# Router rows and expert rows kept as f16 halves and turned by DMA instead of by TensorE

## The chip, the cores and the metric

The kernel runs on one core of a Trainium2 chip. The metric is device time in microseconds (us) from start to end of one execution. Engines are named as in the profile: PE is TensorE's matmul stream and PEld its weight loads, DVE is VectorE, ACT is ScalarE, POOL is GpSimd, SP is SyncE. SP issues most of the plain DMAs; POOL issues the indirect ones.

## What is computed

One decoder layer over 4096 tokens of width 1024: attention and convolution heads with an output projection, then a channel mixer with top-1 of 4 groups and top-2 of 8 experts. The part that the change touches is how the normalized row `hn` of each token reaches the router and the experts.

```
h = h + mixed @ w_out[l]
hn = rms_norm(h, ffn_norm_g[l])
...
g_prob = softmax(xf @ w_gr + b_gr);  g_p, g_idx = top_k(g_prob, 1)
e_logits = einsum('td,dge->tge', xf, w_er) + b_er     # xf is hn in float32
e_val, e_idx = top_k(e_logits of the chosen group, 2)
...
# tokens sorted by expert, in blocks of 128 rows that belong to one expert
def expert_block(args):
    xb, e = args
    return (silu(xb @ w_g[e]) * (xb @ w_u[e])) @ w_d[e]
```

## The kernel before

The kernel has two stages. `mixer` goes over 32 tiles of 128 tokens (loop variable t) and ends with routing; `experts` goes over the blocks of 128 gathered rows (loop variable b), expert by expert. Products keep nearly float32 precision by splitting both factors into a high and a low half and adding three products (hi*hi, hi*lo, lo*hi): f16 halves in the mixer (`split_mm`, L412), fp32r halves in the experts (L1333).

TensorE contracts over the partitions, so every activation has to be turned (transposed) first: 128 tokens on the partitions become 128 features on the partitions. Before the change each turn is made by PE, as four transposes of 128x128 into one PSUM bank, read by ACT for the high half and by DVE for the low half.

**Mixer.** Each engine's program is one `body(t)` written by hand, and its order is the program order. PE's body runs: turn x (psE, psF, L448), scores (psA to psD, L464), router product of the previous tile (psH, 16 small matmuls, L477), q projection (psG), turn the probabilities (L495), k and v (psH), probabilities times V (L520), C projection (psF), H projection (psC), turn a and yc (L535), output projection (psD, psE), counts (L554, L555), B projection (psG), turn k (L568), turn q (psF, psB, L578), turn `hn` (psC, psD, L588). `hn` is made by DVE (L1138) from h (L1134) and a statistic of ACT (L738 to L600). The turned `hn` goes as f16 halves to `both_hnT` (in `wo_all`; ACT L755, DVE L1154), which the router product of the next pass reads. SP stores `hn` as float32 rows of 4 KB in `hn_dram` (L397).

**Experts.** For block b, POOL loads the slot numbers (L1289), gathers the 128 rows from `hn_dram` into `xg` (L1257), and later adds the finished block into the output (`scatter`, L1269). PE's `block_` runs: gate (psA, 24 matmuls), turn of the previous block's activations (psE, L1348), up (psB, 24), turn of the next block's rows (psC, psD, L1341), down of the previous block (psF, psG, 12 each). ACT and DVE share one outline, `halves`: where a new expert begins, split its gate weights; scale the finished block into y; split the up weights; `turn` (halves of the activations); `act_stage` (ACT silu L1440, DVE product L1483); `turn_x` (halves of the next block's rows, ACT L1453, DVE L1493, once `up` has read the old ones); split the down weights. A weight matrix is split in 8 pieces (ACT L1427, DVE L1469), and the gate matmuls of an expert's first block follow the pieces one by one. SP reloads each raw weight buffer (2 MB) once both engines have split it. `hold(eng, sem)` is an increment of a semaphore that nobody waits for.

POOL may overwrite `xg` once PE has turned it (`xgT_ps`), and `scatter(b)` waits for both halves of y and for the last scatter to have landed.

## Time and profile before

| | us |
|---|---|
| median of 3 runs | 2934.15 |
| lowest and highest | 2933.95, 2938.82 |
| profiled execution, its time | 2933.64 |
| profiled execution, its span | 2932.0 |

The span runs from the first to the last instruction of the trace; 1.6 us of the profiled execution's time lie around it. Up to about 1480 us the mixer runs, from about 1500 us the experts. Times in the rows are microseconds from the start of the span unless marked ns. A matmul row's own duration overlaps the next one, so the distance between starts tells what it costs PE.

### The profile page before, as it was taken

Reading aid. Unit: us, or ns where it says so; the run is one execution under the profiler, and the core shown is the slowest. Engines: PE = TensorE matmul, PEld = TensorE weight load, DVE = VectorE, ACT = ScalarE, POOL = GpSimd, SP = SyncE. Lnnn points to the kernel's source line nnn. Section 1 sums busy time; section 2 is a strip of 40 time slices with the busy share of each in tenths; the row PEclk is TensorE's granted clock in tenths of the full one; section 3 lists DMA queues with packets and bytes.
Section 4 is the critical chain, followed back from the end, with each engine's and each line's share of the span. In section 5 each row is a group of like instructions: output and inputs, shape, how many; then the busy total and the mean of one; then the engine's idle time right before and its main releaser. Section 6 shows DMA issues by size and latency. Waiting matters only on the chain. (4 is left out here: it accounts for less than half of the span.)

```text
span 2932.0 us, 51902 instructions
## 1 busy us (share of the span) xinstructions
PE 2833.6 (97%) x15862; PEld 2015.1 (69%) x15863; DVE 1685.4 (57%) x4102; ACT 1424.0 (49%) x3174; POOL 809.2 (28%) x826
## 2 busy tenths in 40 slices
PE   4999999999999999999859999999999999999998
PEld 2565566556556656655538888888888888888886
DVE  5566666666666666666643546645564545356543
ACT  6655454555455455545423445544454444345433
POOL 1122223313222221321212323323322323333222
PEclk9899999999999999999979999999999999999999
DMA  8112112111211211221335667766776756657763
GB/s 291 40 69 79 57 61 79 66 63 68 79 53 65 79 64 57 75 78 50 140 111 162 183 196 222 237 200 195 233 243 194 229 150 197 180 170 232 241 189 57
DMA packets 152747, 398.52 MB, mean 136 GB/s; under 512 B 18027, under 2 KB 18188, under 8 KB 151692
## 3 DMA queue, kind: packets, MB, share of 16 engines
q1 hardware_dynamic: 123868, 309.36, 30.6%
q0 software_dynamic: 28848, 88.77, 13.0%
q8 instruction: 16, 0.26, 0.0%
q14 instruction: 15, 0.12, 0.0%
HBM read 310.20 MB, written 87.88 MB: 136 GB/s over the span
## 5 line engine op out<-in xcount | busy, mean ns | idle before, releaser
L412 PE MATMUL psG<-wi_all,xT_hi 128*128 128x512 f16 x1024 | 308.1, 383 | 0.7 <-DVE xT_lo L944 0.7
L1333 PE MATMUL psB<-up_hi,gT_hi 128*128 128x512 f32 x632 | 254.2, 402 | 0.0
L1333 PE MATMUL psA<-gate_hi,gT_hi 128*128 128x512 f32 x632 | 246.6, 390 | 3.1 <-ACT gT_hi L1453 1.7
L1333 PE MATMUL psB<-up_hi,gT_lo 128*128 128x512 f32 x632 | 247.4, 391 | 0.0
L1257 POOL DMA_INDIRECT xg<-hn_rows,slots x80 | 98.2, 1228 | 539.7 <-DMA slots<-slot_table 394.2
L1333 PE MATMUL psA<-gate_hi,gT_lo 128*128 128x512 f32 x632 | 246.7, 390 | 0.0
L1333 PE MATMUL psA<-gate_lo,gT_hi 128*128 128x512 f32 x632 | 246.3, 390 | 0.0
L1333 PE MATMUL psB<-up_lo,gT_hi 128*128 128x512 f32 x632 | 246.2, 390 | 0.0
L1469 DVE TENSOR_TENSOR down_lo<-wi_all,down_hi 128x512 fp32r<-128x512 f32 x256 | 157.0, 685 | 147.3 <-ACT down_hi L1427 147.3
L1453 ACT ACTIVATE gT_hi<-psC 128x512 fp32r<-128x512 f32 x80 | 47.8, 598 | 383.1 <-PE psC L1341 383.1
L1483 DVE TENSOR_TENSOR act_rows<-psB,gated 128x512 f32<-128x512 f32 x79 | 54.7, 692 | 289.6 <-PE psB L1333 289.6
L837 POOL DMA_INDIRECT slot_table<-entry,slot x64 | 64.8, 1013 | 562.5 <-DVE tok L1126 535.2
L1427 ACT ACTIVATE down_hi<-wi_all 128x512 fp32r<-128x512 f32 x256 | 137.0, 619 | 149.4 <-PE psG L1333 149.4
L738 ACT ACTIVATE dump<-h 128x1024 bf16<-128x1024 f32 x32 | 33.8, 1057 | 339.0 <-DVE h L1134 339.0
L1266 POOL COPY rows_of_y<-slots 128x1 int32<-128x1 int32 x80 | 129.4, 1617 | 247.7 <-DVE y L1476 246.9
L412 PE MATMUL psG<-wi_all,xT_lo 128*128 128x512 f16 x512 | 195.8, 382 | 0.0
L1469 DVE TENSOR_TENSOR gate_lo<-wi_all,gate_hi 128x512 fp32r<-128x512 f32 x256 | 157.0, 685 | 46.0 <-ACT gate_hi L1427 46.0
L412 PEld LDWEIGHTS psG<-wi_all,xT_hi 128*128 128x128 f16 x1024 | 98.7, 98 | 117.3 <-issue 4.5
L652 ACT ACTIVATE prob<-prob,soft 128x256 f32<-128x256 f32 x256 | 127.9, 500 | 80.5 <-DVE soft L976 74.9
L412 PE MATMUL psF<-wi_all,xT_hi 128*128 128x512 f16 x528 | 157.4, 380 | 4.6 <-DVE wi_all L936 4.6
L412 PE MATMUL psC<-wi_all,xT_hi 128*128 128x512 f16 x528 | 157.5, 380 | 0.0
L1469 DVE TENSOR_TENSOR up_lo<-wi_all,up_hi 128x512 fp32r<-128x512 f32 x256 | 156.7, 683 | 1.0 <-ACT up_hi L1427 1.0
(343 smaller groups left out, 7174.9 us busy)
## 6 DMA issues: line engine op xcount, KB each, us to landing
wi_all<-in_w_gate SPq DMA_DIRECT2D x32, 2048.0 KB, 9.4
wi_all<-in_w_up SPq DMA_DIRECT2D x32, 2048.0 KB, 12.8
wi_all<-in_w_down SPq DMA_DIRECT2D x32, 2048.0 KB, 9.2
xt<-in_x SPq DMA_DIRECT2D x32, 512.0 KB, 3.3
um<-u_rows SPq DMA_DIRECT2D x64, 256.0 KB, 2.7
xres<-in_x SPq DMA_DIRECT2D x32, 512.0 KB, 4.1
out_rows<-h SPq DMA_DIRECT2D x32, 512.0 KB, 2.6
hn_rows<-hn SPq DMA_DIRECT2D x32, 512.0 KB, 2.6
```

Source lines behind the costliest of these rows:

```text
L412: m = nc.tensor.matmul(ps, left[l][:, k, :], weights.half(r, k, n, width), start=(k == 0 and j == 0), stop=(k == KD - 1 and j == 2))
L652: s.activation(prob[:, hd, :], prob[:, hd, :], ACT.Exp, bias=ntop[:, hd:hd + 1], accum_out=psum_[:, hd:hd + 1]).then_inc(p_sb.sem, 1)
L738: s.activation(dump[:], h[:], ACT.Square, accum_out=ss_h).then_inc(h_rs.sem, 1)
L837: g.indirect_dma_start(table, bass.IndirectOffsetOnAxis(ap=slot[:, n:n + 1], axis=0), entry[:, n, :], None, bounds_check=E * CAP - 1).then ...
L1257: pool.indirect_dma_start(xg[:], None, hn_dram, bass.IndirectOffsetOnAxis(ap=slots[:, 0, 0:1], axis=0), bounds_check=SEQ + P - 1).then_inc ...
L1266: g.tensor_copy(rows_of_y[:], slots[:, 3, 0:1]).then_inc(named, 1)
L1333: m = nc.tensor.matmul(ps[:, :], l[:, k, :], r[:, r_k[n], :], start=(n == 0 and j == 0), stop=(n == len(l_k) - 1 and j == 2))
L1427: s.activation(hi[n][:, k, :], raw[n][:, k, :], ACT.Copy).then_inc(hi_s[n], 1)
L1453: s.activation(gT_hi[:, 4 * h:4 * h + 4, :].rearrange("p k c -> p (k c)"), ps[:, :], ACT.Copy).then_inc(xgT_hi, 1)
L1469: v.tensor_tensor(lo[n][:, k, :], raw[n][:, k, :], hi[n][:, k, :].bitcast(F32), ALU.subtract).then_inc(lo_s[n], 1)
L1483: v.tensor_tensor(act_rows[:], psB[:, :], gated[:], ALU.mult).then_inc(act_s, 1)
```

## The change

It removes PE's turn of `hn` in the mixer and of the gathered rows in the experts, with the two PSUM reads that followed each, and lets DMA transposes do both, on f16 halves.

- **Mixer, ACT and DVE:** after `hn`, ACT writes its f16 high half over all 1024 columns (into the bytes of `a`), and DVE then the low half (into the bytes of `Cs`). `hn` itself moves behind the k and q copies on DVE; ACT's copy of B (`Bs`) moves behind q and the high half.
- **Mixer, SP:** in place of the store of `hn`, two DMA transposes (high, then low) into `both_hnT`, then two stores of 256 KB each, so a row of `hn_dram` is still 4 KB but holds 1024 high and 1024 low halves. DVE's write of `a` and ACT's write of `Cs` in the next pass wait for all four.
- **Mixer, PE:** the turn of `hn` goes; the turns of k and q come ahead of the B projection; the router product goes behind the q projection and waits for the transposes (`hnT_in`).
- **Experts:** `turn_rows` on ACT, between `turn` and `act_stage`, waits for the gather of the next block and issues two DMA transposes (high, low) from `xg` into `both_gT16`. `turn_x` waits for them (`turned`) and is now one operation of 1024 columns on each engine: ACT scales the high half into `gT_hi`, DVE the low half into `gT_lo`, no longer one after the other. POOL waits for `turned` before it overwrites `xg`.
- One semaphore `held` takes the place of three. `inv_hn` is the inverse of the scale of the halves.

The core of the diff:

```diff
@@ -231,7 +233,7 @@
     mT_hi, mT_lo = sb("mT_hi", [P, KD, P], F16), sb("mT_lo", [P, KD, P], F16)
     h, hn = sb("h", [P, D]), sb("hn", [P, D])
     both_hnT = w_out_split.spare(KD * P).bitcast(F16).rearrange("p (a k c) -> p a k c", a=2, k=KD)
-    hnT_hi, hnT_lo = both_hnT[:, 0], both_hnT[:, 1]
+    hn_hi, hn_lo = a[:].bitcast(F16), Cs[:].bitcast(F16)
...
@@ -393,10 +396,18 @@
             if live(t, 1):
                 after(sp, h_s, t)
                 sp.dma_start(out[bass.ds((t - 1) * P, P), :], h[:]).then_inc(rows_out.sem, 16)
-                after(sp, hn_s, t)
-                sp.dma_start(hn_dram[bass.ds((t - 1) * P, P), :], hn[:]).then_inc(rows_out.sem, 16)
+                after(sp, lg_ps, t - 1)
+                after(sp, hn_hi_s, t)
+                hold(sp, held)
+                sp.dma_start_transpose(both_hnT[:, 0], hn_hi).then_inc(hnT_in.sem, 16)
+                after(sp, hn_lo_s, t)
+                hold(sp, held)
+                sp.dma_start_transpose(both_hnT[:, 1], hn_lo).then_inc(hnT_in.sem, 16)
+                for half, rows in enumerate((a, Cs)):
+                    sp.dma_start(hn_dram[bass.ds((t - 1) * P, P), half * CC:(half + 1) * CC], rows[:]).then_inc(halves_out.sem, 16)
         schedule(sp, body)
         after(sp, rows_out, TILES)
+        after(sp, halves_out, TILES)
 
     @block.tensor
     def _(pe):
...
@@ -456,8 +467,10 @@
 
                     if j == 1:
                         after(pe, qT_dve, t)
-                    if j >= 2:
-                        after(pe, hT_dve, t - 1, j - 1)
+                    if j == 2:
+                        after(pe, u_s, t)
+                    if j == 3:
+                        after(pe, h_s, t - 1, 1)
                     for i in range(2):
                         hd = 2 * j + i
                         for half in range(2):
@@ -468,9 +481,17 @@
                             m = nc.tensor.matmul(ps[:, i * 256:(i + 1) * 256], cst[0:1, C_ONE:C_ONE + P],
                                                  pad_mask, start=False, stop=True)
                     m.then_inc(s_ps.sem, 1)
+            if full:
+                after(pe, b_sb, t)
+                after(pe, xTl, t + 1, 1)
+                split_mm(psG[:, :], xT, "in", 0, False, range(KD // 2))
+            if proj:
+                after(pe, xTl, t + 1)
+            if full:
+                split_mm(psG[:, :], xT, "in", 0, False, range(KD // 2, KD)).then_inc(pq.sem, 1)
             if route:
 
-                after(pe, hT_dve, t - 1)
+                after(pe, hnT_in, t - 1)
                 for k in range(KD):
 
                     for half in ((0, 1) if k < KD - 1 else (1, 0)):
...
@@ -478,14 +499,6 @@
                                              w_rt16[:, k, 0:2 - half, :].rearrange("p a n -> p (a n)"),
                                              start=(k == 0 and half == 0), stop=(k == KD - 1 and half == 0))
                 m.then_inc(lg_ps.sem, 1)
-            if full:
-                after(pe, b_sb, t)
-                after(pe, xTl, t + 1, 1)
-                split_mm(psG[:, :], xT, "in", 0, False, range(KD // 2))
-            if proj:
...
@@ -578,15 +587,10 @@
                         m = nc.tensor.transpose(ps[:, c * P:(c + 1) * P],
                                                 q2[:, 4 * b + c, :, :].rearrange("p a d -> p (a d)").bitcast(F32), ident)
                     m.then_inc(qT_ps.sem, 1)
-            if attn:
-                after(pe, hn_s, t)
-                if proj:
-                    after(pe, u_s, t + 1)
-                for b, ps in enumerate((psC, psD)):
-                    for c in range(4):
-                        k = 4 * b + c
-                        m = nc.tensor.transpose(ps[:, c * P:(c + 1) * P], hn[:, k * P:(k + 1) * P], ident)
-                    m.then_inc(hT_ps.sem, 1)
+            if full:
+                after(pe, q_sq, t + 1)
+                after(pe, q_n, t + 1)
+                split_mm(psG[:, :], xT, "in", O_B).then_inc(pb.sem, 1)
         schedule(pe, body)
...
@@ -707,6 +711,8 @@
             if proj:
                 after(act, pc, t + 1)
                 after(act, u_s, t)
+                after(act, hnT_in, t - 1)
+                after(act, halves_out, t - 1)
                 s.activation(Cs[:], psF[:, :], ACT.Copy, scale=inv_in).then_inc(c_sb.sem, 1)
             if isinstance(t, int) and t == 0:
                 split_hi("out", FIRST_CHUNKS)
@@ -740,20 +746,19 @@
                 after(act, hn_s, t - 1)
                 rstd(h_rs, t, ss_h, ln1[3], r_h, D)
             if full:
+                after(act, qT_ps, t + 1, 1)
+                after(act, s_ps, t)
+                s.activation(qT[:, 0:4 * P], psF[:, :], ACT.Copy).then_inc(qT_act.sem, 1)
+            if attn:
+                after(act, hn_s, t)
+                after(act, mT_ps, t, 1)
+                s.activation(hn_hi, hn[:], ACT.Copy, scale=hn_scale).then_inc(hn_hi_s.sem, 1)
+            if full:
                 after(act, pb, t + 1)
                 after(act, cv, t)
                 if isinstance(t, int) and t == 0:
                     act.wait_ge(band_out, 16 * len(band_places))
                 s.activation(Bs[:], psG[:, :], ACT.Copy, scale=inv_in).then_inc(b_sb.sem, 1)
-                after(act, qT_ps, t + 1, 1)
-                after(act, s_ps, t)
-                s.activation(qT[:, 0:4 * P], psF[:, :], ACT.Copy).then_inc(qT_act.sem, 1)
-            if attn:
-                after(act, lg_ps, t - 1)
-                for b, ps in enumerate((psC, psD)):
-                    after(act, hT_ps, t, b + 1)
-                    s.activation(hnT_hi[:, 4 * b:4 * b + 4, :].rearrange("p k c -> p (k c)"), ps[:, :], ACT.Copy,
-                                 scale=hn_scale).then_inc(hT_act.sem, 1)
             if isinstance(t, int) and t == -2:
                 bounds("in")
...
@@ -1027,6 +1032,8 @@
                 after(dve, o_ps, t)
                 after(dve, den_s, t)
                 after(dve, mT_ps, t - 1)
+                after(dve, hnT_in, t - 1)
+                after(dve, halves_out, t - 1)
                 a_heads = a[:].rearrange("p (h d) -> p h d", h=HEADS)
                 for kv, ps in enumerate((psE, psA)):
                     o = ps[:, :].rearrange("p (h a d) -> p h a d", h=4, a=2)
@@ -1132,10 +1139,6 @@
                     after(dve, h_ps, t, n + 1)
                     c = slice(n * 512, (n + 1) * 512)
                     v.scalar_tensor_tensor(h[:, c], ps[:, :], inv_out, xres[:, c], ALU.mult, ALU.add).then_inc(h_s.sem, 1)
-                after(dve, h_s, t)
-                after(dve, h_rs, t)
-                after(dve, hT_ps, t - 1)
-                v.scalar_tensor_tensor(hn[:], h[:], r_h, g_ffn[:], ALU.mult, ALU.mult).then_inc(hn_s.sem, 1)
             if full:
                 after(dve, k_prev, t + 1)
             if proj:
...
-                for b, ps in enumerate((psC, psD)):
-                    after(dve, hT_act, t, b + 1)
-                    v.scalar_tensor_tensor(hnT_lo[:, 4 * b:4 * b + 4, :].rearrange("p k c -> p (k c)"), ps[:, :], hn_scale,
-                                           hnT_hi[:, 4 * b:4 * b + 4, :].rearrange("p k c -> p (k c)"),
-                                           ALU.mult, ALU.subtract).then_inc(hT_dve.sem, 1)
+                after(dve, h_s, t)
+                after(dve, h_rs, t)
+                after(dve, hn_hi_s, t - 1)
+                v.scalar_tensor_tensor(hn[:], h[:], r_h, g_ffn[:], ALU.mult, ALU.mult).then_inc(hn_s.sem, 1)
+                if proj:
+                    after(dve, u_s, t + 1)
+                after(dve, hn_hi_s, t)
+                v.scalar_tensor_tensor(hn_lo, hn[:], hn_scale, hn_hi, ALU.mult, ALU.subtract).then_inc(hn_lo_s.sem, 1)
 
         schedule(dve, body)
 
         steps = [0]
-        last = sig("last").sem
...
@@ -1198,6 +1203,9 @@
     hi = {n: sb(f"{n}_hi", [P, 8, 512], F32R) for n in raw}
     lo = {n: sb(f"{n}_lo", [P, 8, 512], F32R) for n in raw}
     xg = sb("xg", [P, D])
+    rows_hi, rows_lo = (xg[:, h * DE:(h + 1) * DE].bitcast(F16) for h in range(2))
+
+    both_gT16 = wi_flat[:, 3 * 4096:3 * 4096 + KD * P].bitcast(F16).rearrange("p (a k c) -> p a k c", a=2, k=KD)
     gT_hi, gT_lo = sb("gT_hi", [P, KD, P], F32R), sb("gT_lo", [P, KD, P], F32R)
     gated, act_rows = sb("gated", [P, DE]), sb("act_rows", [P, DE])
...
@@ -1289,7 +1297,7 @@
             pool.dma_start(slots[:, 0, :], table[bass.ds(e * CAP + i * P, P), :]).then_inc(slots_in, 16)
             pool.wait_ge(slots_in, 16 * (b + 1))
             if not (isinstance(b, int) and b == 0):
-                pool.wait_ge(xgT_ps, 2 * b)
+                pool.wait_ge(turned, 32 * b)
                 hold(pool, held)
             gather()
...
@@ -1334,13 +1342,6 @@
                                          stop=(n == len(l_k) - 1 and j == 2))
             return m
 
-        def transpose_rows(b):
-            pe.wait_ge(rows_in, 16 * (b + 1))
-            for h, ps in enumerate((psC, psD)):
-                for c in range(4):
-                    m = nc.tensor.transpose(ps[:, c * P:(c + 1) * P], xg[:, (4 * h + c) * P:(4 * h + c + 1) * P], ident)
-                m.then_inc(xgT_ps, 1)
-
         def turn_act(b):
 
...
                 turn_act(b)
             split_mm(psB, range(KD), (gT_hi, gT_lo), (hi["up"], lo["up"]), list(range(KD)), first, "up", e
                      ).then_inc(up_ps, 1)
-            transpose_rows(b + 1)
             if not static0:
 
...
                 turn(b)
+            if turn_rows:
+                turn_rows(b + 1)
             act_stage(b)
             turn_x(b + 1)
...
@@ -1445,18 +1448,26 @@
             act.wait_ge(y_ps, 2 * b + 2)
             s.activation(aT_hi[:].rearrange("p k c -> p (k c)"), psE[:, :], ACT.Copy).then_inc(aT_hi_s, 1)
 
+        def turn_rows(b):
+
+            act.wait_ge(rows_in, 16 * (b + 1))
+            if not (isinstance(b, int) and b == 0):
+                act.wait_ge(xgT_hi, b)
+                act.wait_ge(xgT_lo, b)
+            for half, rows in enumerate((rows_hi, rows_lo)):
+                hold(act, held)
+                act.dma_start_transpose(both_gT16[:, half], rows).then_inc(turned, 16)
+
         def turn_x(b):
             if not (isinstance(b, int) and b == 0):
                 act.wait_ge(up_ps, b)
-            for h, ps in enumerate((psC, psD)):
-                act.wait_ge(xgT_ps, 2 * b + h + 1)
-                s.activation(gT_hi[:, 4 * h:4 * h + 4, :].rearrange("p k c -> p (k c)"), ps[:, :],
-                             ACT.Copy).then_inc(xgT_hi, 1)
+            act.wait_ge(turned, 32 * (b + 1))
+            s.activation(gT_hi[:], both_gT16[:, 0], ACT.Copy, scale=inv_hn[:]).then_inc(xgT_hi, 1)
 
...
         def turn_x(b):
-            for h, ps in enumerate((psC, psD)):
-                dve.wait_ge(xgT_hi, 2 * b + h + 1)
-                v.tensor_tensor(gT_lo[:, 4 * h:4 * h + 4, :].rearrange("p k c -> p (k c)"), ps[:, :],
-                                gT_hi[:, 4 * h:4 * h + 4, :].rearrange("p k c -> p (k c)").bitcast(F32),
-                                ALU.subtract).then_inc(xgT_lo, 1)
+            if not (isinstance(b, int) and b == 0):
+                dve.wait_ge(up_ps, b)
+            dve.wait_ge(turned, 32 * (b + 1))
+            v.tensor_scalar(gT_lo[:], both_gT16[:, 1], inv_hn[:], None, ALU.mult).then_inc(xgT_lo, 1)
 
```

What stands in a row on three engines. PE in the mixer, end of the tile loop: `wo_all` is the output projection's weight and `wi_all` the input projection's, `q` and `kn` are normalized queries and keys. Before, and then after:

```order
L412 MATMUL psG<-wi_all,xT_lo 128x512
L130 REGISTER_ALU
L568 MATMUL psH<-cst,kn 128x128 x2
L578 MATMUL psF<-cst,q 128x128 x4
L578 MATMUL psB<-cst,q 128x128 x4
L588 MATMUL psC<-cst,hn 128x128 x4
L588 MATMUL psD<-cst,hn 128x128 x4
```

```order
L423 MATMUL psE<-wo_all,mT_lo 128x512
L130 REGISTER_ALU
L577 MATMUL psH<-cst,kn 128x128 x2
L587 MATMUL psF<-cst,q 128x128 x4
L587 MATMUL psB<-cst,q 128x128 x4
L423 MATMUL psG<-wi_all,xT_hi 128x512 x2
L423 MATMUL psG<-wi_all,xT_lo 128x512
```

The eight transposes of `hn` are gone, and the B projection (psG) now comes last in the tile, right ahead of the next tile's turn of x.

PE in the experts, the end of `up` and the start of `down` in a block that opens an expert; before, and then after:

```order
L1333 MATMUL psB<-up_hi,gT_lo 128x512
L1338 ISA
L1341 MATMUL psC<-cst,xg 128x128 x4
L1341 MATMUL psD<-cst,xg 128x128 x4
L1333 MATMUL psF<-down_hi,aT_hi 128x512
```

```order
L1341 MATMUL psB<-up_hi,gT_hi 128x512
L1341 MATMUL psB<-up_lo,gT_hi 128x512
L1341 MATMUL psB<-up_hi,gT_lo 128x512
L1356 REGISTER_ALU
L1341 MATMUL psF<-down_hi,aT_hi 128x512
```

The turn of the next block's rows between the two products is gone.

ACT in the same block, from the up weights to the down weights; before, and then after:

```order
L1427 ACTIVATE up_hi<-wi_all 128x512 x8
L1445 REGISTER_ALU
L1446 ACTIVATE aT_hi<-psE 128x512
L1437 REGISTER_ALU
L1440 ACTIVATE gated<-psA 128x512
L1452 ISA
L1453 ACTIVATE gT_hi<-psC 128x512
L1452 REGISTER_ALU
L1453 ACTIVATE gT_hi<-psD 128x512
L1409 REGISTER_ALU
L1427 ACTIVATE down_hi<-wi_all 128x512 x8
```

```order
L1430 ACTIVATE up_hi<-wi_all 128x512 x8
L1448 REGISTER_ALU
L1449 ACTIVATE aT_hi<-psE 128x512
L1453 REGISTER_ALU
L1455 REGISTER_ALU
L1459 DMA_TRANSPOSE wi_all<-xg 128x8x128 x2
L1443 ACTIVATE gated<-psA 128x512
L1464 REGISTER_ALU
L1465 ACTIVATE gT_hi<-wi_all,inv_hn 128x1024
L1410 REGISTER_ALU
L1430 ACTIVATE down_hi<-wi_all 128x512 x8
```

Two DMA transposes stand between the halves of the activations and the silu, and one wide copy takes the place of two.

## Rows read from the trace of the kernel before

**Rows 1.** The page, part 1: busy us, share of the span, instructions.

```profile
PE 2833.6 (97%) x15862; PEld 2015.1 (69%) x15863; DVE 1685.4 (57%) x4102; ACT 1424.0 (49%) x3174; POOL 809.2 (28%) x826
```

**Rows 2.** Windows (mixer, experts): length, busy us per engine, PE clock, DMA share, GB/s.

```profile
200.00:627.00 427.00, 427.00 (x2820) 254.95 (x2817) 276.32 (x877) 225.90 (x597) 111.74 (x100) 1.00 0.18 68
1980.00:2445.00 465.00, 465.00 (x2209) 386.67 (x2207) 247.60 (x395) 212.18 (x395) 144.55 (x160) 1.00 0.71 211
```

**Rows 3.** Chain of waits, one block of the experts: start us, us, what.

```profile
2167.12 5.44 PE psA L1333 x24
...
2173.00 5.49 PE psB L1333 x24
2178.49 0.44 PE psC L1341 x4
...
2179.37 2.75 PE psF L1333 x12
...
2184.84 1.36 PE psA L1333 x6
```

**Rows 4.** Timeline, end of one mixer tile: start us, us, engine, instruction, idle before.

```profile
708.17 1.61 DVE L1138 SCALAR_TENSOR_TENSOR hn<-h,stat,g_ffn 128x1024 f32<-128x1024 f32 x1 [1.84 <-ACT stat L600]
...
710.77 0.69 ACT L747 ACTIVATE Bs<-psG,scale_w 128x512 f32<-128x512 f32 x1 [2.68 <-PE psG L412]
...
711.66 0.60 PE L588 MATMUL psC<-cst,hn 128*128 128x128 f32 x4
...
712.53 0.60 PE L448 MATMUL psE<-cst,xt 128*128 128x128 f32 x4
...
715.32 0.63 PE L477 MATMUL psH<-w_rt,wo_all 128*128 128x72 f16 x16
...
715.80 0.59 PE L412 MATMUL psG<-wi_all,xT_hi 128*128 128x512 f16 x2
```

**Rows 5.** DMA issues: queue, count, KB each, median us to landing.

```profile
u_rows<-u SPq DMA_DIRECT2D x33, 256.0 KB, 2.0
...
xg<-hn_rows,slots POOLq DMA_INDIRECT x80, 4.5
out_rows<-y,rows_of_y POOLq DMA_INDIRECT x80, 9.7
```

**Rows 6.** Groups by line: instructions, busy us, mean ns, idle before, releaser.

```profile
L588 PE MATMUL psC<-cst,hn 128*128 128x128 f32 x128 | 19.3, 273 | 4.0 <-DVE hn L1138 4.0
L738 ACT ACTIVATE dump<-h 128x1024 bf16<-128x1024 f32 x32 | 33.8, 1057 | 339.0 <-DVE h L1134 339.0
```

**Rows 7.** Timeline, experts: ACT, DVE and POOL.

```profile
1779.72 1.11 POOL L1257 DMA_INDIRECT xg<-hn_rows,slots  x1 [7.66 <-DMA slots<-slot_table]
...
2173.12 0.60 ACT L1446 ACTIVATE aT_hi<-psE 128x512 fp32r<-128x512 f32 x1 [1.10 <-PE psE L1348]
...
2181.61 4.28 ACT L1427 ACTIVATE gate_hi<-wi_all 128x512 fp32r<-128x512 f32 x8 [1.55 <-issue]
...
2182.53 4.91 DVE L1469 TENSOR_TENSOR gate_lo<-wi_all,gate_hi 128x512 fp32r<-128x512 f32 x8 [1.64 <-ACT gate_hi L1427]
...
2185.20 1.37 POOL L1257 DMA_INDIRECT xg<-hn_rows,slots  x1 [6.60 <-DMA slots<-slot_table]
```

**Rows 8.** Chain of waits, the block in which the 1779.72 gather falls.

```profile
1777.19 5.44 PE psA L1333 x24
```

**Rows 9.** Issues of the down weights on SP: ns min/median/max, first and last start.

```profile
L170 SPq DMA_DIRECT2D wi_all<-in_w_down x32: 372/373/4075, 1442.3 to 2846.3; - x32
```

**Rows 10.** Timeline, the last tile's turn and router product.

```profile
1478.45 0.66 PE L588 MATMUL psC<-cst,hn 128*128 128x128 f32 x4 [3.96 <-DVE hn L1138]
...
1481.43 0.90 PE L477 MATMUL psH<-w_rt,wo_all 128*128 128x72 f16 x16 [1.57 <-DVE wo_all L1154]
```

**Rows 11.** Chain of waits, first gathered rows to first gate product.

```profile
1510.38 1.11 PE psC L1341 x4
...
1513.81 1.62 PE psA L1333 x3
```

More of the change, by code:

```diff
@@ L488, in body @@
                 split_mm(psG[:, :], xT, "in", 0, False, range(KD // 2, KD)).then_inc(pq.sem, 1)
+            if route:
+                after(pe, hnT_in, t - 1)
+                for k in range(KD):
+                    for half in ((0, 1) if k < KD - 1 else (1, 0)):
+                        m = nc.tensor.matmul(psH[:, 256:256 + (2 - half) * RT], both_hnT[:, half, k, :],
+                                             w_rt16[:, k, 0:2 - half, :].rearrange("p a n -> p (a n)"),
+                                             start=(k == 0 and half == 0), stop=(k == KD - 1 and half == 0))
+                m.then_inc(lg_ps.sem, 1)
             if attn:
@@ L823, in body @@
                     after(pool, v_cur, t)
-                    hold(pool, pool_held)
+                    hold(pool, held)
                     g.tensor_copy(V[:, 0, :], V[:, 1, :]).then_inc(v_prev.sem, 1)
@@ L827, in body @@
                 after(pool, v_st, t + 1)
-                hold(pool, pool_held)
+                hold(pool, held)
                 g.tensor_copy(V[:, 1, :], vst[:]).then_inc(v_cur.sem, 1)
@@ L834, in body @@
                 after(pool, rt2, t - 1)
-                hold(pool, pool_held)
+                hold(pool, held)
                 for n in range(2):
@@ L968, in body @@
                     after(dve, s_ps, t, j + 1)
-                    hold(dve, dve_held)
+                    hold(dve, held)
                     for i in range(2):
@@ L1187, in experts @@
 def experts(nc, ctx, env):
-    out, table, hn_dram, cst, ident, blocks_of, raw, raw_in, load_expert = (env[n] for n in (
-        "out table hn_dram cst ident blocks_of raw raw_in load_expert").split())
+    out, table, hn_dram, cst, ident, blocks_of, inv_hn, held, wi_flat, raw, raw_in, load_expert = (env[n] for n in (
+        "out table hn_dram cst ident blocks_of inv_hn held wi_flat raw raw_in load_expert").split())
     psA, psB, psC, psD, psE, psF, psG = (env[f"ps{c}"] for c in "ABCDEFG")
```

44 lines of the change are left out of this document (19 added, 25 removed).

## The prediction

> **What bounds the kernel now.** I read the busy shares first: PE is busy for 97% of the span, no other compute engine for more than 57% [rows 1]. The windows say whether that holds stage by stage: in a mixer stretch of 427 us PE is busy for 427.00, in an experts stretch of 465 us for 465.00, at full clock [rows 2]. PE has no gap, so each matmul taken away shortens the run, as long as nothing that hung on it comes late. What must not come late is read from the chain of waits and the timelines.
>
> The chain of one block of the experts is PE alone: gate, turn of the activations, up, turn of the next rows, down; from one gate to the next it is 2184.84 - 2167.12 = 17.72 us [rows 3]. The turn of the next rows takes 2179.37 - 2178.49 = 0.88 us of them. In the mixer the turn of `hn` takes 712.53 - 711.66 = 0.87 us of a tile, and PE goes on without a gap [rows 4].
>
> **What is removed.** The experts have 80 turns of rows, one per gather [rows 5]; the first of them is waited for and is costed below with the start. 79 x 0.88 = 69.5 us lie in the chain. The mixer has 128 transposes into psC, four a tile, so 32 turns [rows 6]; the last is exposed and goes below too. 31 x 0.87 = 27.0 us. The PSUM reads that followed on ACT and DVE are replaced by wide operations and were beside PE's work.
>
> **What the DMA transposes need in the experts.** A transpose of 256 KB is not in this trace. I call X the time from the issue of the pair to the landing of both. Nearest rows: a plain store of 256 KB lands in 2.0 us, the gather of 512 KB into SBUF, in the same stretch beside the weight loads, in 4.5, the scatter that adds 512 KB in 9.7 [rows 5]. So 2.0 to 9.7; I take 4.5, since the gather moves the bytes of a pair to the same side, beside the same loads.
>
> When is the pair issued? It stands on ACT behind `turn`, which starts 2173.12 - 2167.12 = 6.0 after the gate's start and takes 0.6 [rows 7]. It also waits for the gather: in one block that was issued 0.4 after the gate's start, in another 2.5 (1779.72 against 1777.19) [rows 3, 7, 8], so the rows are there at 4.9 or 7.0. I take 7.0. When must it have landed? The period becomes 17.72 - 0.88 = 16.84. The wide copy on ACT costs 1.06, by an ACT operation of 1024 columns [rows 6]; DVE's copy now runs beside it. For a block of the same expert X may be 16.84 - 1.06 - 7.0 = 8.8. Where the next block opens an expert, ACT then goes through 1.55 of loop overhead and the first piece of the gate split, and DVE follows: 1.55 + (2182.53 - 2181.61) + 4.91/8 = 3.1 [rows 7]; X may be 5.7. There are 31 such blocks (32 loads per weight [rows 9], less the first expert) and 48 of the other kind. At 4.5 both are met: cost nothing, hidden under up and down.
>
> What queues behind the new instructions on ACT: the silu, which only the product after up needs, at about 10.9 after the gate's start by the chain (2178.49 less 2167.12 is 11.4, when up is read). Two issues at 0.37 each are nothing; but SP was once held 4.08 in an issue when its queue was full [rows 9]. Two such holds would end the silu at 7.0 + 8.2 + 0.6 = 15.8 and the wide copy at 16.9: nothing is lost within an expert, 3.1 where one opens. One hold costs nothing. POOL waits for the pair before its next gather; that gather is issued at 17 to 20 after this gate, so it sees X only above 10.
>
> **In the mixer.** ACT's high half starts when `hn` ends, 708.17 + 1.61 = 709.8, and takes 1.06; DVE's low half takes at most 1.61 more: 712.5 [rows 4, 6]. The router product now stands behind the q projection. The next tile's turn of x starts at 711.66; turn and scores take 715.32 - 712.53 = 2.79 [rows 4], 24 matmuls of 512 columns at most 5.44 as in the experts [rows 3]: the router product is due at 719.9. From the first issue that leaves 9.0 us, from the second 7.4. At 4.5 it costs nothing. The B projection now ends right before the turn of x, and the q projection overwrites its bank: ACT's copy (0.69, row 710.77) has 2.79 us of turn and scores as cover [rows 4]; without cover it would be 0.7 a tile. On SP the load of the next x and residual tile queue behind the transposes and stores; ACT reads x only some three projections later, about 16 us. The new waits for the stores stand on operations of the next tile's middle, as far away.
>
> **The two exposed turns.** Last tile: before, from the turn of `hn` to the router product 1481.43 - 1478.45 = 3.0 us [rows 10]. After: 1.06 + 1.61 + the low half's landing, 2.0 to 4.5, 3.2 taken: 5.9, so +2.9 (+1.7 to +4.2). Start of the experts: before, from rows landed to the gate product 1513.81 - 1510.38 = 3.4 [rows 11]. After: X + 1.06 = 5.6, so +2.1 (0 to +7.4).
>
> **Sum,** against the profiled execution's own time of 2933.6 (the median of the runs is 2934.15, half a microsecond more): 2933.6 - 69.5 - 27.0 + 2.9 + 2.1 = 2842.1 us, 3.1% less.
>
> **A page against the change.** The rows show PE's turn at 0.11 us per 128x128 (0.44 for four) [rows 3]. The Trainium skill (VectorE: DVE Perf Modes, The three transpose paths) gives 1309 ns for one 128x128 by DMA against 390 on TensorE, and its rules say to use TensorE where PSUM is a good destination. By an estimate from that page, sixteen in a row would be 20.9 us a block. Another page (Advanced Engine Details and Errata, X-Bar Transpose (TRN2)) says that transpose DMAs on this chip are as fast as regular ones, by which the sum above stands. No row here decides between them.
>
> **Rivals.**
> 1. *X between the limits.* Beside two weight loads (DMA share 0.71 in the experts [rows 2]) the pair lands in 5.7 to 8.6. Only the 31 blocks that open an expert stall, by X - 5.7 each. At 7.1: 31 x 1.4 = 43, 2885 us. For it speaks the load; against it, that the gather has 4.5 in the same load.
> 2. *Slower than before.* The DMA engines, not PE, bound the block: cost 31(X - 5.7) + 48(X - 8.8) against 91.5 gained. The point from which it decides is X = 8.7. At the scatter's 9.7: 31 x 4.0 + 48 x 0.9 = 167, 3009 us. For it: the scatter row. Against it: the scatter reads, adds and writes.
> 3. *Piece by piece.* The transposes are worked off one after the other at small pieces, each of the pair as long as the scatter: X = 19.4. Experts: 31 x 13.7 + 48 x 10.6 = 934. Mixer: landing at 710.9 + 19.4 = 730.3 against 719.9, 31 x 10.4 = 322. In all 4098 us. [...] Against it only that no DMA row of this size is so slow.
> 4. *The mixer gives nothing.* The new order (B projection last, router late) makes PE wait 0.87 a tile: 2842 + 27 = 2869 us. Against it: a cover of 2.79 over 0.69.
>
> **How the numbers follow.** Forecast 0.62 (2834 to 2852), rival 1 0.16, rival 2 0.12, rival 3 0.05, rival 4 0.05. The predicted time is the forecast's, 2842. The range goes from 2833 (both exposed turns at their lower bounds, a few us of further slack) to 2895 (rival 4 and rival 1 up to X = 7.4); what is left out, X above 7.4, is about 0.2. Within 0.2%, about 6 us and what a measurement of this kernel can tell from no change, lies only X near 8.6: 0.02. Faster 0.82, which is the forecast, rival 4 and nearly all of rival 1; slower 0.16.
>
> **What would show it.** In the chain of one block: up followed by down with nothing between, 16.84 from gate to gate, no idle ahead of the gate product. In the issue table: the transposes landing in 2 to 5.7 us. On ACT: the wide copy released by the end of up, not by the DMA. In the mixer: tiles 0.87 shorter, PE without a gap at the router and q products. Wrong: PE idle ahead of psA in blocks that open an expert (rival 1), in all blocks (rival 2), PE idle at the router product (rival 3), or a wait for `Bs` at psG (rival 4).

## The result, and the profile of the changed kernel

The changed kernel takes 3319.6 us (median of 4 runs, 3310.1 to 3329.5) against 2934.4 for the kernel before: the ratio is 1.131, with a 95% interval of 1.127 to 1.135. It is 385 us slower than before, where the forecast was 92 us faster. The profiled execution has a span of 3327.8 us.

Busy shares, as in [rows 1], from the page of the changed kernel:

```profile
PE 2844.9 (85%) x14966; PEld 1986.7 (60%) x14967; DVE 1666.2 (50%) x3990; ACT 1428.8 (43%) x3062; POOL 836.0 (25%) x826
```

PE runs 896 instructions fewer than before, as planned, but is busy for 85% of the span instead of 97%. The windows (length, PE busy, granted clock, DMA share, GB/s), the same two stretches as in [rows 2], say where:

```profile
200.00:627.00 427.00, 427.00 (x2817) 1.00 0.26 83
...
1980.00:2445.00 465.00, 372.42 (x1525) 0.88 0.73 181
```

In the mixer PE still has no gap. In the experts it is busy for 372 of 465 us and its granted clock is 0.88, so for part of the time it is at the lower of its two levels (1.2 and 2.4 GHz). The waits say for what (engine, line, waited for: total us, times, longest):

```profile
POOL xg L1265 <- DMA wi_all<-xg: 732.1, 73, 18.0
...
ACT gT_hi L1465 <- DMA wi_all<-xg: 474.8, 63, 15.7
ACT gated L1443 <- issue: 439.0, 78, 11.3
...
PE psA L1341 <- ACT gT_hi L1465: 358.8, 46, 32.9
```

`wi_all<-xg` is the pair of DMA transposes. The gate product waits for ACT's wide copy, and that for the pair. The chain of waits through one expert of two blocks, to be read beside [rows 3] (the longer pieces of it):

```profile
2200.66 0.45 PE psE L1349 x4
...
2201.47 1.34 ACTq L1459
...
2202.91 8.31 DMA wi_all<-xg
...
2212.95 0.64 ACT gate_hi L1430
...
2214.45 7.34 PE psA L1341 x24
2221.79 0.45 PE psE L1349 x4
...
2222.60 1.25 ACTq L1459
...
2223.97 15.25 DMA wi_all<-xg
2239.24 1.16 ACT gT_hi L1465
...
2240.44 8.10 PE psA L1341 x24
```

From one gate product to the next it is 2240.44 - 2214.45 = 25.99 us, where 16.84 was forecast. Up and down no longer stand in the chain: they end under the pair's 16.6 us (issue 1.25, landing 15.25). The 24 matmuls of the gate product take 7.34 and 8.10 us after such a wait, 5.44 in [rows 3]. That slow clock is a consequence of the waits: PE is busy for 2844.9 us here, against 2733.0 in the run of experiment 2 where the same matmuls have almost no wait ahead of them.

### The profile page after: what moved, and what is told of

It reads as the page before. It is cut to its first block, busy times and chain, and to the rows that moved or that the text cites. A ratio compares the mean times of both kernels' runs of the same rounds, so it can differ in the third digit from the quotient of the medians.

```text
span 3327.8 us, 50496 instructions
## 1 busy us (share of the span) xinstructions
PE 2844.9 (85%) x14966; PEld 1986.7 (60%) x14967; DVE 1666.2 (50%) x3990; ACT 1428.8 (43%) x3062; POOL 836.0 (25%) x826
## 4 chain that ended last, share of the span: by engine, by line
DMA 25%; PE 23%; ACTq 3%; ACT 2%; issue 1%; DVE 0%; POOL 0%; POOLq 0%; DVEq 0%
DMA wi_all<-xg 25%; PE psA L1341 16%; PE psB L1341 3%; ACTq L1459 2%; ACT gT_hi L1465 2%; PE psG L1341 1%; PE psF L1341 1%; PE psE L1349 1%; DVE gate_lo L1480 0%; ACT gate_hi L1430 0%; ACTq L1231 0%; ACTq L1230 0%; DMA out_rows<-y,rows_of_y 0%; DMA xg<-hn_rows,slots 0%; ACT up_hi L1430 0%
## 5 line engine op out<-in xcount | busy, mean ns | idle before, releaser
L1341 PE MATMUL psA<-gate_hi,gT_hi 128*128 128x512 f32 x632 | 295.9, 468 | 407.7 <-ACT gT_hi L1465 358.8
L1341 PEld LDWEIGHTS psA<-gate_hi,gT_hi 128*128 128x128 f32 x632 | 142.9, 226 | 465.2 <-ACT gT_hi L1465 378.4
L1465 ACT ACTIVATE gT_hi<-wi_all,inv_hn 128x1024 fp32r<-128x1024 f16 x80 | 92.0, 1150 | 505.9 <-DMA wi_all<-xg 474.8
L1265 POOL DMA_INDIRECT xg<-hn_rows,slots x80 | 88.7, 1109 | 809.6 <-DMA wi_all<-xg 732.1
L1341 PE MATMUL psA<-gate_lo,gT_hi 128*128 128x512 f32 x632 | 283.7, 449 | 0.0
L1341 PE MATMUL psA<-gate_hi,gT_lo 128*128 128x512 f32 x632 | 280.5, 444 | 0.0
L1494 DVE TENSOR_TENSOR act_rows<-psB,gated 128x512 f32<-128x512 f32 x79 | 54.6, 692 | 447.7 <-ACT gated L1443 241.8
L1505 DVE TENSOR_SCALAR gT_lo<-wi_all,inv_hn 128x1024 fp32r<-128x1024 f16 x80 | 60.2, 752 | 420.7 <-DMA wi_all<-xg 420.7
L1274 POOL COPY rows_of_y<-slots 128x1 int32<-128x1 int32 x80 | 150.4, 1880 | 388.5 <-DVE y L1487 387.9
L1443 ACT ACTIVATE gated<-psA 128x512 f32<-128x512 f32 x79 | 47.3, 599 | 442.6 <-issue 439.0
L1341 PEld LDWEIGHTS psA<-gate_hi,gT_lo 128*128 128x128 f32 x632 | 141.2, 223 | 34.9
```

The lines of the kernel that those rows point to most:

```text
L1265: pool.indirect_dma_start(xg[:], None, hn_dram, bass.IndirectOffsetOnAxis(ap=slots[:, 0, 0:1], axis=0), bounds_check=SEQ + P - 1).then_inc ...
L1274: g.tensor_copy(rows_of_y[:], slots[:, 3, 0:1]).then_inc(named, 1)
L1341: m = nc.tensor.matmul(ps[:, :], l[:, k, :], r[:, r_k[n], :], start=(n == 0 and j == 0), stop=(n == len(l_k) - 1 and j == 2))
L1443: s.activation(gated[:], psA[:, :], ACT.Silu).then_inc(silu_s, 1)
L1465: s.activation(gT_hi[:], both_gT16[:, 0], ACT.Copy, scale=inv_hn[:]).then_inc(xgT_hi, 1)
L1494: v.tensor_tensor(act_rows[:], psB[:, :], gated[:], ALU.mult).then_inc(act_s, 1)
```

## Why the row I leaned on was not beside the loads

The prediction took 4.5 us for the pair because the gather takes 4.5 "beside the same loads". Whether it ran beside them is told by the times of issue. In the kernel before, the timeline of SP and then of POOL for the same block:

```profile
2157.41 0.37 SPq L170 DMA_DIRECT2D wi_all<-in_w_up  x1
2172.97 0.37 SPq L170 DMA_DIRECT2D wi_all<-in_w_down  x1
2187.66 0.37 SPq L170 DMA_DIRECT2D wi_all<-in_w_gate  x1
2193.06 0.37 SPq L170 DMA_DIRECT2D wi_all<-in_w_up  x1
```

```profile
2178.00 0.60 POOL L1289 DMA_DIRECT2D slots<-slot_table  x1 [0.83 <-POOL slots L1277]
2185.20 1.37 POOL L1257 DMA_INDIRECT xg<-hn_rows,slots  x1 [6.60 <-DMA slots<-slot_table]
```

This gather goes out 12.2 us after the down load and 2.5 us ahead of the next gate load. The strip of the 16 DMA engines from 2140 to 2220, 2 us a digit, has it:

```profile
DMA  9997038799999993099996036699999932799994
GB/s 410 307 277 152 0 45 248 203 339 260 244 293 410 385 321 137 2 270 391 281 246 121 0 53 240 180 406 357 380 292 246 318 151 47 256 291 385 291 221 83
```

The slice that ends at 2186 is a 0: the gather starts on idle DMA engines. It is like this for all: none of the 80 gathers had a load issued in the 7.9 us ahead of it. In 44 cases a load was issued behind the gather, within 4.5 us. The waits show the reason: the gather waits for a slot list of 1 KB, and that list is itself issued some 5 us behind the load (2178.00 against 2172.97) and is slow to land beside it. The row has waits for the list in total, times, and the longest:

```profile
POOL xg L1257 <- DMA slots<-slot_table: 394.2, 57, 8.6
```

So what the gather waits for has mostly waited out the loads. The pair has no such guard. By [rows 7] it is issued some 7 us after the gate product's start, and by the SP rows above the loads go out at 5.9 (down, 2172.97 - 2167.12) or at 2.8 and 8.2 (gate and up, against the gate product of 2184.84 in [rows 3]). So every pair but those of third blocks had to meet one load or two. The trace of the kernel before could have told that, though these SP rows were not among the rows of the prediction.

## The experiments

A pair's time, in the text and the table below, is read from the timelines, from the issue of its first transpose to the start of ACT's wide copy.

**1. The mixer's part alone.** The experts stay as before; `hn` is stored in one piece of float32 as before.

```diff
                 sp.dma_start_transpose(both_hnT[:, 1], hn_lo).then_inc(hnT_in.sem, 16)
-                for half, rows in enumerate((a, Cs)):
-                    sp.dma_start(hn_dram[bass.ds((t - 1) * P, P), half * CC:(half + 1) * CC], rows[:]).then_inc(halves_out.sem, 16)
+                sp.dma_start(hn_dram[bass.ds((t - 1) * P, P), :], hn[:]).then_inc(rows_out.sem, 16)
```

> The change in the mixer alone: halves turned by DMA on SP for the router, TensorE order of the change; hn still stored as float32 rows and the experts as before (TensorE turns the gathered rows). In the changed kernel the first gather of the experts starts at 1481.95 us, 23.6 us earlier than before. Theory (the mixer's part works as forecast, the loss is all in the experts): 2934 - 24 = about 2910 us, no stall of PE at the router product. Rival (the two stages are not separate: halves stored by two more stores, or transposes on SP, cost something that shows only here): above 2925 us.

Measured: 2911.6 us (2910.3 to 2917.1), ratio 0.992 [0.991, 0.994] to 2935.1: 23.5 us or 0.8% faster, as the theory had it. All of the loss is in the experts. This is the only version here with all of its work done that beats the kernel before.

**2. The changed kernel with its loads almost gone, and the kernel before likewise.** The loads of experts 1 to 31 are issued and waited for, but move 64 KB each instead of 2 MB; the products then use mostly the first expert's weights.

```diff
-            sp.dma_start(dst, w[0, bass.ds(e, 1)].rearrange("o (k p) n -> p (o k) n", p=P)).then_inc(raw_in[n], 16)
+            src = w[0, bass.ds(e, 1)].rearrange("o (k p) n -> p (o k) n", p=P)
+            if not isinstance(e, int):
+                dst, src = dst[:, 0:1, 0:128], src[:, 0:1, 0:128]
+            sp.dma_start(dst, src).then_inc(raw_in[n], 16)
```

> The changed kernel with the weight loads of experts 1 to 31 cut to 128 partitions x 512 bytes each (that part of the computation is left out, all instructions on the engines stay). Theory A (the transposes of the experts land late because they share the DMA engines with the weight loads): a pair lands in about 4.5 us as in the mixer (3.1 us for one, 1.25 us between the two issues), PE has no gap, the clock stays at full, about 2842 us, as the blind sum had it. Rival B (a transpose on ACT's queue is slow by itself, or behind gather and scatter): landing stays near 8.7 us and the time above 3200 us.

> Control: the kernel before with the same cut of the weight loads (that part of the computation is left out). PE has no gap before, so both theories expect 2934 us within 0.3%. A shorter time would mean that the loads also slow other things.

Measured: 2840.8 us for the changed kernel, 2932.9 for the one before. The chain of waits of the former:

```profile
2099.87 1.82 PE psA L1344 x8
2101.69 0.44 PE psE L1352 x4
2102.13 5.49 PE psB L1344 x24
2107.62 2.72 PE psF L1344 x12
2110.34 2.72 PE psG L1344 x12
2113.06 5.44 PE psA L1344 x24
```

This is the chain that was forecast, up followed by down with nothing between. The sum's terms for PE hold once the loads are gone. The control, 2932.9 us, lies within the runs of the kernel before (2931.2 to 2940.0), so no cost of the loads shows there. ACT's copy waits for the end of the up product here, so 5.2 us is an upper bound of the pair's time. The windows of the experts' middle, for the kernel before, for it with the small loads, and for the changed kernel with the small loads:

```profile
1980.00:2445.00 465.00, 465.00 (x2209) 1.00 0.71 211
```

```profile
1980.00:2445.00 465.00, 465.00 (x2209) 1.00 0.31 64
```

```profile
1980.00:2445.00 465.00, 465.00 (x2107) 1.00 0.51 99
```

The loads take 0.71 - 0.31 = 0.40 of the DMA engines' time, the transposes 0.51 - 0.31 = 0.20. At the forecast's pace the changed kernel would want 0.51 + 0.40 x 17.72/16.84 = 0.93 of it. There was capacity left, but little. Whether the order of issue then decides what is late is the question of experiments 5 and 6.

**3. Does the size of the loads' pieces matter?** Loads split by columns, so that rows arrive in runs of 1 KB and a transpose could slip in more often.

```diff
+            for part in range(parts):
+                c = slice(part * 256, (part + 1) * 256)
+                sp.dma_start(dst[:, :, c], src[:, :, c]).then_inc(raw_in[n], 16)
```

> The changed kernel with every weight load cut in column parts of 256 float32, so that its contiguous runs are 1 KB in place of 2 KB (gate, up) and 4 KB (down); same bytes, same computation. The transposes of the experts move 42 MB in 168960 packets of 248 bytes. Theory A1 (the DMA engines take the queues in turn packet by packet, so that each small packet of a transpose waits for one large packet of a load): shorter load packets let a pair land sooner, median landing of one transpose from 8.7 to about 5 us, time about 3050 to 3200 us although the loads themselves get no faster. Rival A2 (the engines share by bytes, or the sum of bytes decides): landing unchanged or longer, time 3320 us or more.

Measured: 3269.0 us, 50 less than the changed kernel, and between what theory A1 (3050 to 3200) and rival A2 (3320 or more) expected. Pairs beside two loads took 16.3 us in the mean, against 19.3 in the changed kernel; those beside the down load took no less than there. So the size of a piece is at most a small part of the loss.

**4. Half the bytes of gate and up.** The edit is that of 2 with `dst[:, 0:4], src[:, 0:4]`, and was meant to cut every load of experts 1 to 31 to 1 MB, with stale weights in the other half. The down weights are laid out in four parts and not in eight, so for them 0:4 is everything. The issue table has it:

```profile
wi_all<-in_w_down SPq DMA_DIRECT2D x32, 2048.0 KB, 10.6
wi_all<-in_w_gate SPq DMA_DIRECT2D x31, 1024.0 KB, 5.3
wi_all<-in_w_up SPq DMA_DIRECT2D x31, 1024.0 KB, 6.5
```

> The changed kernel, weight loads of experts 1 to 31 cut to half (1 MB each); the products then use stale halves, so the output is wrong in value but the work is the same. Theory Q: a pair beside two loads lands in about 5.2 + (19 - 5.2)/2 = 12 us, beside one in 7.3; only opening blocks stall, by about 12 - 5.7 = 6.3, 31 x 6.3 = 195: 3040 us (2950 to 3120). Rival T (a load's presence, not its bytes, is what slows a pair): pairs as in the changed kernel, 3250 to 3330.

Measured: 3112.4 us. Pairs beside gate and up, which were halved, took 11.6 us (mean of 30; 12 expected) instead of 19.3. So the bytes count, and rival T is out by 140 us. Pairs just behind the down load took 11.9, not the 7.3 expected, since that load was still whole. That they took more than the 10.7 of the changed kernel goes with their place: 26 were issued only 0.7 to 2.5 us behind it, and took 12.4 in the mean; the five that were issued 3 us or more behind it took 9.5. In the changed kernel the same split gives 12.0 (13 pairs, 1.5 to 3 us behind) and 9.8 (17 pairs, over 3 us). So the time since the load's issue counts as well. What a half down load costs was not run.

**5. The same bytes in another order.** Here only the time of issue moves. SP waits, ahead of each load, for pairs that have landed; a group of three numbers says for which pair gate, up and down wait: 1 for none that is still to come, 2 for the pair that the opening block issued, 3 for the one behind it. `opened` is the number of blocks ahead of the expert at work.

```diff
+            opened = sp.value_load(blocks_of[0:1, bass.ds(e + (E - 1), 1)], min_val=0, max_val=3 * TILES)
-            for n in raw:
+            for n, pairs in zip(raw, (2, 2, 3)):
                 sp.wait_ge(hi_s[n], 8 * e)
                 sp.wait_ge(lo_s[n], 8 * e)
+                sp.wait_ge(turned, 32 * (opened + pairs))
                 load_expert(sp, n, e)
```

> The changed kernel; only the time at which the weight loads of the next expert are issued moves: gate and up wait until the pair of transposes that the expert's opening block issued has landed, down until the pair after that. The same bytes move. Theory Q (a pair lands when the loads already in flight have drained; what counts is what was issued before it): the opening block's pair meets no load and lands within 5.2 us; the second pair meets the end of up, about 11 us, and the next expert's opening pair the down load, about 9 to 10. Stalls of 3 to 4 us for two pairs of an expert, 31 experts, and some for the later weights: 3050 us (2970 to 3150), the clock nearer to full. Rival R (any load in flight at any time slows a pair by the same, since the engines are simply short of capacity: shares of 0.51 without the loads and 0.40 for the loads): ordering gains nothing, 3270 to 3340, or more since the loads come later.

> As the run before, but only the gate load goes after the opening pair; up and down go after the next one. Theory Q: the second pair meets no load (5.2 us), but the next opening pair meets the end of up and down, about 15, so the wait moves instead of going, and the up weights come late: 3100 us (3030 to 3250). Rival R: 3270 to 3400.

The second has (2, 3, 3). Measured: 2949.5 and 2989.9 us, beside 2939.6 for the kernel before. An order alone gives back 370 of the 385 us, with the same bytes and transposes; rival R is out. Both are faster than theory Q had them (3050 within 2970 to 3150, and 3100 within 3030 to 3250): in the first, the loads have drained before the later pairs are issued, where pairs of 9 to 11 us were expected. There 78 of 79 pairs were issued with no load just ahead, and took 5.3 us in the mean. The rest, 2949.5 - 2842 = 107 us, is lost in another place. Three pieces of this kernel's chain of waits, and two rows of ACT's timeline:

```profile
2126.79 6.83 DMA slots<-slot_table
...
2134.62 7.64 DMA xg<-hn_rows,slots
...
2144.03 3.67 DMA wi_all<-xg
```

```profile
2103.49 3.47 ACTq L1461 DMA_TRANSPOSE wi_all<-xg  x2
2107.06 0.60 ACT L1445 ACTIVATE gated<-psA 128x512 f32<-128x512 f32 x1 [7.44 <-issue]
```

Now the slot list and the gather stand behind gate and up (the gather takes 7.3 us, 4.5 before), and the rows come late: of the 7.44 us in which ACT stands still ahead of the silu, 3.47 are the transposes' issue, and the other 3.9 come before it. Second blocks issue their pair 10.9 to 11.5 us after the gate product's start (means), where 7.0 was taken. The wait has moved one transfer upstream.

**6. Two orders between.** (1, 2, 3) lets the gate load go at once, (1, 2, 2) the down load too.

> The changed kernel; the gate load is issued as soon as its buffer is free, as there, the up load after the opening block's pair has landed, the down load after the pair behind it. Theory Q: the opening pair meets the rest of one load (up to 9.4 us against a limit of 8.8), the later ones none (5.2); the slot list and the gather of the pair behind meet one load instead of two, so that pair is no longer issued late; 2870 us (2845 to 2910). Rival G (the engines are near their capacity, 0.93 of the time, and every order only moves the late transfer, as in the run with both loads after the opening pair, 2949): 2930 to 3000.

> As the run before, but the down load too is issued as soon as its buffer is free, ahead of the next expert's opening pair. Theory Q: pairs where an expert opens meet one load of 2 MB issued a little earlier, 9 to 10 us against a limit of 5.7: 31 x 4 = 120 us more than the run before, 2990 (2940 to 3060). Rival G: about the same as the run before, within 20 us.

Measured: 2956.9 us (2952.1 to 2963.3), ratio 1.008 [1.007, 1.010], and 3092.1. For (1, 2, 3) rival G was right (2930 to 3000) and theory Q's 2870 was not: it is no better than (2, 2, 3). Letting the down load go ahead of the second block's pair costs 135 us, near the 120 of theory Q, though the total lies above its range (2940 to 3060); those pairs take 12.0 us. The pairs of opening blocks say what a load issued behind a pair does. With the gate load ahead of them and up held back they took 10.4 and 9.2 us (means of 30), and 19.3 in the changed kernel, where up goes out 1.4 us behind them. The DMA share in the experts for (1, 2, 3):

```profile
1980.00:2445.00 465.00, 433.58 (x1906) 0.99 0.82 230
```

At 0.82 each of the four orders had some transfer late, whichever went first. None of them beats the kernel before.

**7. The traffic without anyone waiting.** The kernel before keeps its turns on PE and issues, beside them, two transposes a block on ACT's queue from a spare region to another one. The rows are zeros and the result is thrown away.

```diff
+        def idle(b):
+            act.wait_ge(idle_set, 1)
+            if not (isinstance(b, int) and b == 0):
+                act.wait_ge(idle_turned, 32 * b)
+            act.wait_ge(rows_in, 16 * (b + 2))
+            for half in range(2):
+                hold(act, held)
+                act.dma_start_transpose(idle_out[:, half], idle_rows[:, half * 512:(half + 1) * 512].bitcast(F16)).then_inc(idle_turned, 16)
```

> The kernel before, which still turns its rows on PE, with two extra transposes of 256 KB a block on ACT's queue, from and to a spare region, that no computation waits for. It does 80 pairs of transposes too many, and its output is the same. Theory W (the loss is PE's wait for a pair's landing; the traffic and the hold of ACT are cheap): ACT is held 3 to 10 us from about 7 us after the gate's start, its copies for the next gate are late by a few us only where an expert opens; 2950 us (2934 to 3040). Rival C (the traffic itself is too much: the loads and gathers come late for everything): 3200 us or more.

Measured: 3163.9 us, 224 more than the 2939.6 of the kernel before. Neither theory had it: it is far above theory W's 2950 and a little below rival C's 3200. The waits of PE:

```profile
PE psC L1344 <- DMA xg<-hn_rows,slots: 186.9, 31, 23.9
```

and two pieces of its chain:

```profile
2079.48 12.11 DMA slots<-slot_table
...
2092.56 7.55 DMA xg<-hn_rows,slots
```

A slot list of 1 KB takes 12.11 us to land here, and the gather behind it 7.55. This is not so for every block: the median of the lists is 3.7 us (6.2 before). But in 30 of the 31 waits the list was issued some 4 us behind the up load, and the gather went out 10.9 to 18.0 us after the list. Nobody waits for the idle transposes, but small transfers beside them and a load are late. The waits (less 23 us at the start, which the kernel before has too) and the slower clock (PE is busy for 2898.5 us instead of 2833.6) about make up the 224. Ahead of the list in the chain stand DVE's split of the gate weights and its half of y, and these may be late through ACT's hold in the issues (550.9 us ahead of `gated`); this run doesn't part the two.

## Why the prediction was wrong, step by step

**PE bounds the kernel, each turn taken away shortens it.** Right as long as no transfer is late: 2840.8 us with small loads against 2842.1 by the sum.

**The mixer's terms** (-27.0 and +2.9). Right in their sum. The first gather of the experts starts 23.6 us earlier, against a forecast of 24.1. That gather's line, before and after (duration ns min/median/max, first and last start):

```profile
L1257 POOL DMA_INDIRECT xg<-hn_rows,slots x80: 1065/1106/1908, 1505.6 to 2889.1; - x80
```

```profile
L1265 POOL DMA_INDIRECT xg<-hn_rows,slots x80: 1064/1067/1442, 1482.0 to 3285.3; - x80
```

Rival 4 fell with it: PE keeps its 427.00 of 427.

**X, the pair's time.** This is the step that failed. 4.5 us was taken for all blocks from the gather's row. Measured, by what was issued from some 5 us ahead of the pair on:

| beside the pair | pairs | mean X, us | limit of the prediction | gate to gate, us | by the limit |
|---|---|---|---|---|---|
| no load (third blocks; the last blocks) | 17 | at most 5.2 | 5.7 (15 of them), 8.8 | 17.2 | 16.8 |
| the down load, about 3 us ahead; the next block opens an expert | 16 | 10.4 | 5.7 | 22.4 | 21.5 |
| the down load, about 3 us ahead; a third block follows | 15 | 11.1 | 8.8 | 20.6 | 19.1 |
| gate about 4 ahead, up 1.4 behind (opening block) | 30 | 19.3 | 8.8 | 27.9 | 27.3 |

The last column is 16.84 + X - limit, where X is above it. The limits were nearly sound: the blocks took 0.4 to 1.5 us more. With these X the prediction's own formula gives 2842 + 16 x 4.7 + 15 x 2.3 + 30 x 10.5 + 4 for the start = 3271 us, and 3319.6 was measured (3329.5 in the profiled execution, from which the table is read). The rest is what the last two columns differ by, about 58 us over these blocks. It goes with the slow clock: the gate product takes 7.34 us or more instead of 5.44, so the pair goes out 8.8, 8.4 and 7.4 us after its start (means of the last three rows), where 7.0 was taken. For experiment 4 the formula gives 3076 against 3112, for (1, 2, 2) 3009 against 3092, for (1, 2, 3) 2929 against 2957, for (2, 3, 3) 2913 against 2990, and for (2, 2, 3) 2846 against 2949. It is too low each time, since it knows neither late rows nor the slow clock. The error of the prediction was thus of two kinds: a single X for classes of blocks that meet different loads, and a price from a transfer that avoids the loads.

**Rival 2** named the place and the direction (the DMA engines bound the block, from a mean X of 8.7 on). Its price of 9.7 stopped at the scatter's median. The measured 19.3 is rival 3's value, though not for rival 3's reason: in the mixer, beside few other transfers, a transpose lands in 3.1 us (median of each of SP's two lines) and a pair in the experts within 5.2; it isn't slow by itself. With this falls the estimate from the Trainium skill (VectorE: DVE Perf Modes, The three transpose paths) in the prediction: sixteen blocks one after the other at 1309 ns would be 20.9 us a pair at any time. The rule that transpose DMAs are as fast as regular ones (the Trainium skill, Advanced Engine Details and Errata, X-Bar Transpose (TRN2)) is not borne out either: with few other transfers a transpose of 256 KB lands in 3.1 us, against 2.0 for the plain store of 256 KB in [rows 5] and 2.3 to 2.4 for those of the changed kernel's mixer.

**What queues behind the issues.** I took one issue at 0.37 us and allowed two holds of 4.08 on ACT. From the issue to the silu it was 7.5 us in the median beside the down load, 5.1 beside two, and 2.8 with none. One transposing issue takes 1.25 us at the least, not the 0.37 of a plain one:

```profile
L1459 ACTq DMA_TRANSPOSE wi_all<-xg x160: 1252/1378/10205, 1486.9 to 3298.0; - x160
...
DMA to landing us min/median/max: 3.1/8.7/22.4
```

The silu was late for that, and DVE waited for it (`DVE act_rows <- ACT gated`, 241.8 us in 33 waits), which was in no step of mine. PE hardly felt it: its waits for the turned activations' halves come to 1.8 us.

**POOL** was to see X only above 10. That was wrong. POOL waited for the pair 73 times, 732.1 us in all, and that includes most third blocks, whose pair takes 5.2 us. With the small loads of experiment 2 there are 19 such waits and PE has no gap. Behind the long pairs the next gather came late as well.

**The start of the experts** (+2.1). It was +6.1: the rows landed at 1486.82, the gate product began at 1496.40. That is within the bounds given (0 to +7.4).

**The clock** was in no step. Ahead of 62 of the gate products PE now stood still, up to 14.4 us and once, at the start of the experts, 32.9 (407.6 us in all), and its granted clock in the experts fell to 0.88; with the loads made small it is 1.00. PE's busy time grew by 2844.9 - 2733.0 = 112 us, some of it under the pairs' time. It couldn't have been a term at X = 4.5, but it belonged to rivals 1 and 2.

## What to carry to other kernels

Before a transfer's duration is taken as a price for another one, look at what else was in flight when it ran, and at what it waited for: a transfer that follows another transfer may have been timed by the queue to run on empty engines, and then it shows their price only. Place the new transfer's issue on the same time axis as each large load, class of block by class of block, and price each class by the bytes ahead of it and by how long ago they were issued. And where transposes move from PE to the DMA engines, add up the engines' shares first: at 0.7 used and 0.2 asked for, the order of issue decided here between losses of 0.3% and of 13%, and the forecast gain of 3% came only with the loads made small.

## What the runs showed of the hardware that I had not expected

- A pair of transposes of 256 KB each (0.5 MB) takes about 0.51 x 16.84 - 0.31 x 17.72 = 3.1 us of all sixteen DMA engines, by the windows with small loads and the time of a block in each. The loads take 0.40 of the window of 465 us, in which 33 of them were issued: 5.6 us for each 2 MB. Both are estimates from these windows. Byte for byte the transposes are about twice as dear. In the middle of the mixer, where the DMA share is 0.26 with them, PE has no gap.
- A pair lands after the load issued ahead of it has drained, and a load issued 1.5 us behind the pair's first issue delays it too. The down load of 2198.16 landed 8.5 us later, at 2206.7, and the pair issued at 2201.47 was there at 2211.2. The up load of 2224.14 landed at 2239.0, and the pair of 2222.60 at 2239.2. The strip of the changed kernel from 2180 to 2260, 2 us a digit, has this second pair in a full block of nines:

```profile
DMA  9999810703999994170089999999911703999994
```

- This holds across queues: the loads are on SP's queue, the transposes on ACT's, the slot list on POOL's. Which stage is shared, the DMA engines or something behind them, these runs don't tell, and it stays open.
- An issue of a DMA transpose holds its engine for 1.25 us with free queues, and up to 10.2 us in the changed kernel. A plain issue on SP took 0.37 in the same stretch.
